# Prompt attention of a hybrid decoder step: transpositions and value products in groups of up to four quads, three PSUM banks for turned quads and one for the value sums

## The reference, cut to what matters

```python
def nsa_core(q, pos_q, gates, kc, vc, pos_c, ks_blk, vs_blk, kw, vw, pos_w, ovl):
    p_c = masked_softmax(jnp.einsum('bgrqd,bgnd->bgrqn', q, kc), pos_c[None, :] <= pos_q[:, None])
    o_c = jnp.einsum('bgrqn,bgnd->bgrqd', p_c.astype(vc.dtype), vc)
    ...
    p_s = masked_softmax(jnp.einsum('bgrqd,bgqkd->bgrqk', q, k_sel), m_s.reshape(B, G, 1, Tq, -1))
    o_s = jnp.einsum('bgrqk,bgqkd->bgrqd', p_s.astype(v_sel.dtype), v_sel)
    ...
    p_w = masked_softmax(jnp.einsum('bgrqd,bgkd->bgrqk', q, kw), m_w)
    o_w = jnp.einsum('bgrqk,bgkd->bgrqd', p_w.astype(vw.dtype), vw)
    return gates[..., 0:1] * o_c + gates[..., 1:2] * o_s + gates[..., 2:3] * o_w
```

## Time and profile before

| | |
|---|---|
| median of 3 runs | 2297.04 us (2295.06 to 2297.14) |
| span of the profiled execution | 2298.0 us |
| PE busy in the span | 2131.9 us (93%) |
| the stage of this case | from about 697 to 1010 us of the span |
| PE, DVE, ACT busy in that stage | 301.8, 201.3, 162.9 us of 313.0 |
| granted PE clock in that stage, mean | 0.98 |

### The profile page before, as it was taken

One profiled execution on the slowest core, in us unless ns is written; L12 is line 12 of the kernel. 1 busy time (PEld: TensorE's weight loads), 2 busy tenths in 40 slices (PEclk: granted clock), 3 DMA queues, 4 the chain that ended last, 5 costly groups with the idle time before them and its releaser, 6 DMA issues. The chain is left out here.

```text
span 2298.0 us, 46326 instructions
## 1 busy us (share of the span) xinstructions
PE 2131.9 (93%) x18884; PEld 1523.2 (66%) x18884; DVE 899.7 (39%) x2082; ACT 523.8 (23%) x1474; POOL 562.4 (24%) x641
## 2 busy tenths in 40 slices
PE   8999999898888999998997999999999999898976
PEld 6446664587775666656676888884568777667732
DVE  2015344355456666634543634332564111111111
ACT  2211111233334554533331111110111111111100
POOL 1027112122230111130023534442211222222212
PEclk9999999999978999999998999999989999999999
DMA  5001040000050000046546122214567999999997
GB/s 186 30 32 42 16 158 2 1 2 2 26 89 5 1 1 2 2 96 189 159 129 166 28 55 65 55 38 131 194 245 276 365 367 376 368 366 367 364 380 262
DMA packets 169602, 323.96 MB, mean 141 GB/s; under 512 B 34207, under 2 KB 102312, under 8 KB 169182
## 3 DMA queue, kind: packets, MB, share of 16 engines
q1 hardware_dynamic: 149270, 293.02, 36.8%
q0 software_dynamic: 12096, 21.43, 3.9%
q10 hardware_dynamic: 8016, 6.46, 0.9%
HBM read 302.03 MB, written 40.36 MB: 149 GB/s over the span
## 5 line engine op out<-in xcount | busy, mean ns | idle before, releaser
L428 PE MATMUL psum<-w,hT 128*128 128x512 f32 (+1 forms) x512 | 201.7, 552 | 0.0
L428 PE MATMUL psum<-hT,w 128*128 128x344 f32 x576 | 169.1, 454 | 0.0
L428 PEld LDWEIGHTS psum<-w,hT 128*128 128x128 f32 x512 | 97.1, 193 | 96.3 <-issue 89.2
L1628 ACT ACTIVATE a_P<-psum,a_nmax 128x512 f32<-128x512 f32 (+4 forms) x256 | 122.8, 493 | 126.1 <-DVE a_nmax L1524 72.6
L428 PEld LDWEIGHTS psum<-hT,w 128*128 128x128 f32 x576 | 108.8, 190 | 56.9 <-ACT dnT L479 0.9
L1520 DVE TENSOR_REDUCE a_nmax<-psum 128x2 f32<-128x1024 f32 (+4 forms) x128 | 91.5, 737 | 82.2 <-PE psum L1429 55.0
L2846 PE MATMUL psum<-f_wg,f_xT 128*32 128x384 f32 x864 | 97.6, 487 | 9.3 <-DMA f_wg<-w_gate 8.4
L2780 POOL DMA_INDIRECT f_x<-h_rows,tokens x36 | 37.7, 1048 | 272.6 <-PE psum L2831 174.3
L2846 PE MATMUL psum<-f_wu,f_xT 128*32 128x384 f32 x864 | 97.4, 487 | 5.5 <-DMA f_wu<-w_up 5.4
L2848 PE MATMUL psum<-f_wg,f_xT 128*32 128x128 f32 x864 | 98.6, 273 | 0.0
L2848 PE MATMUL psum<-f_wu,f_xT 128*32 128x128 f32 x864 | 98.5, 273 | 0.0
(11 more groups left out here) (629 smaller groups left out, 4481.7 us busy)
## 6 DMA issues: line engine op xcount, KB each, us to landing
f_wg<-w_gate SPq DMA_DIRECT2D x64, 1024.0 KB, 21.2
f_wu<-w_up SPq DMA_DIRECT2D x64, 1024.0 KB, 22.1
f_wd<-w_down SPq DMA_DIRECT2D x64, 1024.0 KB, 21.8
k_stage<-cache_nsa SPq DMA_DIRECT2D x128, 192.0 KB, 2.5
w<-w_in SPq DMA_DIRECT2D x6, 2048.0 KB, 8.2
x_wg<-w_in SPq DMA_DIRECT2D x16, 512.0 KB, 5.1
x<-x_prompt SPq DMA_DIRECT2D x8, 512.0 KB, 6.1
o_w<-w_out SPq DMA_DIRECT2D x2, 2048.0 KB, 8.3
```

Of the source, the lines that this page charges most:

```text
L428: ins = nc.tensor.matmul(PS[i % 4][0:m_rows, 0:n], lhsT, rhs, start=(k == 0), stop=(k == KD - 1))
L1628: ins = nc.scalar.activation(Pb[u % 2][:, g, o:o + w], S[n % 2][:, g, col:col + w], ACT.Exp, bias=nmax[:, u % 2, c0 + g:c0 + g + 1], accum ...
```

## The change

Within a segment, quads are taken in groups of up to four (`GROUP = 4`; no segment has more than four entries, so a group is a whole segment here). PE turns the whole group, then issues the scores of the next unit's segment, then the products of the group before. Turned quads go round three banks (`PS[4]`, `PS[5]`, `PS[7]`), and the value sums of all units use one bank, `PS[6]`, so that the first product of a unit waits until the unit before has been finished. ACT now copies every second quad of a segment, and DVE the others and the gates. On ACT all its copies of a group stand ahead of the exponentials, as its one copy did before. On DVE the copies of a group now stand ahead of the maxima; `finish(u - 1)` follows the maxima, and `scales(u)` comes last.

```diff
+    GROUP = 4
...
+        turn_banks = (PS[4], PS[5], PS[7])
+        NTB = len(turn_banks)
+        products = PS[6]
...
-        on_act = [n == 0 and q is not None for u, k, n, q in stream]
+        on_act = [n % 2 == 0 and q is not None for u, k, n, q in stream]
...
+        def groups(u, k):
+            fs = in_segment(u, k)
+            return [fs[n:n + GROUP] for n in range(0, len(fs), GROUP)]
...
-                if f >= 2:
-                    pe.wait_ge(act_pt if on_act[f - 2] else dve_pt, copied[f - 2])
-                bank = PS[4 + f % 2]
+                if f >= NTB:
+                    pe.wait_ge(act_pt if on_act[f - NTB] else dve_pt, copied[f - NTB])
+                bank = turn_banks[f % NTB]
...
-                if k == 0 and n == 0 and u >= 2:
-                    pe.wait_ge(fin_done, u - 1)
+                if k == 0 and n == 0 and u >= 1:
+                    pe.wait_ge(fin_done, u)
...
+            turned = []
             for u in range(NU):
                 for k in range(2):
-                    for n, f in enumerate(in_segment(u, k)):
-                        turn(f)
+                    for n, group in enumerate(groups(u, k)):
+                        for f in group:
+                            turn(f)
                         if n == 0 and u + 1 < NU:
                             score(u + 1, k)
-                        weigh(f - 2)
-            weigh(len(stream) - 2)
-            weigh(len(stream) - 1)
+                        for f in turned:
+                            weigh(f)
+                        turned = group
+            for f in turned:
+                weigh(f)
...
             for u in range(NU):
                 for k in range(2):
-                    if u + 1 < NU:
-                        maxima(u + 1, k)
-                    for f in in_segment(u, k):
-                        if not on_act[f]:
-                            copy_quad(dve, f)
+                    for n, group in enumerate(groups(u, k)):
+                        for f in group:
+                            if not on_act[f]:
+                                copy_quad(dve, f)
+                        if n == 0:
+                            if u + 1 < NU:
+                                maxima(u + 1, k)
+                            if k == 0 and u:
+                                finish(u - 1)
                     if k == 0:
                         scales(u)
-                        if u:
-                            finish(u - 1)
...
-                    for f in in_segment(u, k):
-                        if on_act[f]:
-                            copy_quad(act, f)
-                    if u + 1 < NU:
-                        exps(u + 1, k)
+                    for n, group in enumerate(groups(u, k)):
+                        for f in group:
+                            if on_act[f]:
+                                copy_quad(act, f)
+                        if n == 0 and u + 1 < NU:
+                            exps(u + 1, k)
```

More of the change, by code:

```diff
@@ L1449, in weigh @@
             def weigh(f):
-                if f < 0 or stream[f][3] is None:
+                if stream[f][3] is None:
                     return
@@ L1462, in weigh @@
                         v, first, last = R[:, kt, c:c + 64], kt == (0, window(i))[branch - 1], kt == i
-                    ins = nc.tensor.matmul(PS[6 + u % 2][64 * g:64 * g + 64, branch * P:(branch + 1) * P], v,
+                    ins = nc.tensor.matmul(products[64 * g:64 * g + 64, branch * P:(branch + 1) * P], v,
                                            PT[real[f] % RING][0:keys, x * P:(x + 1) * P], start=first, stop=last)
@@ L1485, in copy_quad @@
             engine.wait_ge(tp_done, f + 1)
-            src = PS[4 + f % 2]
+            src = turn_banks[f % NTB]
             done = act_pt if on_act[f] else dve_pt
@@ L1549, in finish @@
                     dve.wait_ge(o_done, u - 1)
-                nc.vector.tensor_tensor(part_o[u % 2], PS[6 + u % 2][:, 0:3 * P], Bt[u % 2], ALU.mult).then_inc(fin_done, 1)
+                nc.vector.tensor_tensor(part_o[u % 2], products[:, 0:3 * P], Bt[u % 2], ALU.mult).then_inc(fin_done, 1)
             x = kv_cmp[0:NCP, 0, :].rearrange("p (g d) -> p g d", d=HD)
```

## The result

The changed kernel takes 2329.78 us (median of 4 runs, 2326.78 to 2331.13), the kernel before 2297.09 on the same chip (4 runs, 2295.06 to 2299.88): a ratio of 1.0127, 95% interval 1.0111 to 1.0142. The change makes the kernel 1.3% slower. The forecast was 2323 with a range of 2306 to 2345.

The account below looks back on a forecast made before the run. PE was taken to set the stage's pace, busy 301.8 of 313 us. Waits of +21, with removed gaps included, plus 6 for the clock make 27 on 2298.0: 2324 for the median, stated as 2323, range 2306 to 2345.

Parts of the forecast that it names:

- The ring: Gates' turn awaits ACT's copy behind exponentials, whose scores await the previous group: 14.9 us a unit at i = 7.
- The gates' wait: At i = 7, PE idles some 2.3 us before it can turn the gates, the fourth entry of segment 1.
- the fourth quad's: At i = 7, PE idles 1.1 us before turning the fourth quad of segment 0, waiting for ACT's copy.
- By blocks: Stage by units 0-8, 8-16, 16-24, 24-31: +11.5, -1.2, +1.8, +5.2 us; with the start, +21.
- The 4: Ahead of the first mark, the ring's waits at the lower clock: between 0.7 and 4 us, taken as 4.
- The clock: PE's idle time at i 7 and 6 lowers the granted clock in most of eight units: 0 to 14 us, taken as 6.
- Rival 2: Clock falls in all units with i of 4 and up: 27 us instead of 6, 2345; with a longer ring, chance 0.15.
- The removed gaps: PE's switches between turns and products: some 200 gaps of 0.17 us go, 34 us gained if PE never waits.
- Rival 1: The gain comes: PE stays the pace, 34 us saved, 2263 us, if the first quad's copy is ready; chance 0.08.
- The small units: From i = 2 down, gates wait for DVE's finish, now ahead of scales: 7.4, 6.5 and 5.7 us a unit.
- the chain from finish to scales: At small i, last product through finish and scales to the gates being laid out: 2.3 us, 2.1 above i = 0.
- Things that cost nothing: the single product bank: Finish of the unit before is done before the gates' turn, so the first product does not wait: no cost.

Follow-up runs that it names:

- run 8: Changed kernel plus matmuls of constants on PE ahead of the gates' turn and fourth quad, to keep it at work: 2323.8 us, 1.0101 of the kernel before.
- run 1: Changed kernel with segment 1's scores issued ahead of the gates' turn and DVE's gates copy behind the maxima: 2283.96 us, 0.9933 of the kernel before.
- run 2: As run 1, with segment 0's fourth quad also turned behind the scores: 2277.1 us, 0.9899 of the kernel before.
- run 3: Changed kernel with copies swapped: DVE takes first and third quads, ACT second and fourth: 2290.7 us, 0.9960 of the kernel before.
- run 4: Changed kernel with scales ahead of finish on DVE, as before the change: 2321.72 us, 1.0092 of the kernel before.
- run 5: Changed kernel with groups of one entry (GROUP = 1): 2350.98 us, 1.0228 of the kernel before.
- run 6: Changed kernel with groups of two entries (GROUP = 2): 2332.58 us, 1.0146 of the kernel before.
- run 7: Changed kernel with groups of three entries (GROUP = 3): 2315.19 us, 1.0066 of the kernel before.
- run 10: As run 5, with two banks for turned quads and two for value sums: 2346.64 us, 1.0200 of the kernel before.
- run 11: As run 5, with each product two turns behind its own instead of one: 2306.72 us, 1.0035 of the kernel before.
- run 12: As run 2, with two banks for turned quads and two for value sums: 2343.21 us, 1.0181 of the kernel before.

## Why the prediction was right

**The ring** held, by its place and by its length. Where no fall of the clock disturbs it, a unit of `i = 6` takes 14.14 us (14.2 predicted), one of `i = 5` 11.97 (12.0), of `i = 4` 11.05 and 11.28 (11.05), of `i = 2` 7.35 (7.4), of `i = 1` 6.27 (6.5). At `i = 7` the changed kernel's shortest is 15.2, and run 8, at full clock, has 14.84 and 14.90, for 14.9. The gates' wait at `i = 7` is 2.30 us in the unit shown, predicted as some 2.3; the fourth quad's, predicted as 1.1, is 0.73 to 1.03 in three units (726.64, 791.29, 805.43) and not there in the four in which PE had just worked at half clock and came late enough to find the bank free. Runs 1, 2 and 3 remove the ring in three ways, by order and by engine, and each makes the kernel faster than the one before.

**By blocks.** The first mark came 1.95 us earlier than before, because the half clock of the stage's start ended at 711 us and not at 717, as far as the runs show: run 1, whose half clock ended at 717, has the same DVE order in this place and its mark at 23.2. So I count from the second scores that are issued while unit 0 is turned. They start 22.8 us into the stage before and 24.3 after: the start cost 1.5 us, not 4. The 4 was for the lower clock, and where that lasts as long as before, in run 4, the same scores start 26.9 us into the stage, 4.1 later. From there to the mark of unit 8 it is 17.1 us more in the changed kernel, 9.1 without the clock's 8.0 (11.5 predicted); then -0.2 (-1.2), +2.4 (+1.8), and +11.1, 5.5 without the clock (+5.2 predicted); and 1.1 at the end, all of it clock. Together 33.0 in the stage. The waits are 18.4 of it, for the 21 that I had, and the clock 14.6, for 6.

**The clock** is the term that was mis-sized: "most of eight units", 6 us, and nothing at the end. It fell in four units of `i` 7 and 6, which cost 8.0 (2.0 each, where 1.7 was estimated), and again in the last three units, which cost 6.7 with what follows them. I had looked for falls only where PE idles for 2 us and more. That the total came out within 7 us is in small part luck: a start that was cheaper and waits that were shorter than predicted made up for a third of what the clock cost more. Rival 2, a fall in every unit of `i` 4 and up, did not come: block 8-16 is at full clock throughout, with gates' waits of 0.8 to 1.49 us. The Trainium skill ("TensorE: Matmul & The Clock Gate", Part 4, PE-mode transpose) says that transpositions don't count as activity. The trace speaks against it here: in the kernel before, PE does nothing but transpositions from 626 to 636 us, and the clock rises from 0.51 (625 to 632) to 1.00 (632 to 636) while it does.

**The removed gaps** were counted rightly and priced a little too high: 34 us for 200 switches were predicted, and run 2 shows 21 to 24 for 161. By the rows of the weight loads they went in the changed kernel too, where the time shows as PE's idle time. **Rival 1,** that the gain comes, is what runs 1 and 2 are: it hung on the copy being there when the fourth entry is due, and a change of order by one entry does that, not a faster copy. Its 2263 was too low, in part since a turn behind the scores brings switches back. **The small units:** the chain from finish to scales was right (run 4 takes it away and is 10.8 us shorter in the last two blocks, 5.2 of it the chain and the rest the clock that it frees).

**"Things that cost nothing: the single product bank"** is right for the changed kernel: no product waits for `finish` there. Its reason was right too narrowly. It holds because a whole segment's turns and scores lie between a unit's last product and the next one's first; runs 5 to 7, where I took it over to smaller groups, missed by 37 to 56 us. In run 5 the larger part is the lag (runs 10 and 11); in runs 6 and 7 the shares of lag, bank and ring stay open.

What stays open is how much of the 66 us of run 12 is clock: it has seven stretches at 0.50 behind 720 us, and no run kept PE at work there.

## What to carry to other kernels

When an in-order engine's work is put in groups, count for every entry which buffer it needs, who frees it, and whether that releaser waits for something that this engine issues only behind the group: the first such entry is a ring, and moving that one entry behind the issue was worth more here (46 us, run 1 against the changed kernel) than all the saved switches. The largest wait in the list may only cover the next one. Run 10 removed 29.8 us of waits and won 4.3. A producer's lag in turns (here from turn to product) has to be kept when groups get smaller, since it hides the copy between them.

## What the hardware showed that I had not expected

The granted clock fell to 0.50 in the last three units, behind a wait of 1.22 us (1016.96) in a unit of 6 us, and stayed there until 1049, past the stage's end, with PE busy for 7.16 of 8 us. Longer waits did not bring it down each time: the gates' waits of 1.76 us (768.04) and 1.75 (812.48) were followed by half clock, those of 1.75 at 784.20 and 798.34 were not, nor any of the 1.49 to 0.80 us in `i` 5 and 4. The same wait of unit 0 was followed by half clock in run 8 (3.38 us) and not in the changed kernel (3.40 us), so that the length of a wait alone does not tell. Some 50 us of the stage behind 730 us were at the half clock, and they cost some 15; PE had idle time in each unit that could take up a part of the rest.
